# DeltaNet heads of a 1-core transformer kernel: the triangular inversion on packed 64x64 blocks, keys left unscaled

## The reference, cut to what matters

```python
def l2norm(t):
    return t * lax.rsqrt(jnp.sum(t * t, axis=-1, keepdims=True) + EPS)

def gated_delta_scan(q, k, v, g, beta, s0, with_output):
    ...   # q is l2norm(q) * 128 ** -0.5, k is l2norm(k)
    gc = jnp.cumsum(to_chunks(g), axis=-1)
    decay = jnp.exp(jnp.where(incl, gc[..., :, None] - gc[..., None, :], -jnp.inf))
    kb = kc * bc[..., None]
    lmat = jnp.where(pos[:, None] > pos[None, :],
                     jnp.einsum('nbhid,nbhjd->nbhij', kb, kc) * decay, 0.0)
    rhs = jnp.concatenate([vc * bc[..., None], kb * jnp.exp(gc)[..., None]], axis=-1)
    sol = lax.linalg.triangular_solve(lmat, rhs, left_side=True, lower=True, unit_diagonal=True)
    ...
    def step(s, inp):
        v_new = u_i - jnp.einsum('bhcd,bhde->bhce', w_i, s)
        s_next = s * gl_i[..., None, None] + jnp.einsum('bhcd,bhce->bhde', kd_i, v_new)
        ...   # o = qd_i s + qk_i v_new
def finish(o, z):
    o = o * lax.rsqrt(jnp.mean(o * o, axis=-1, keepdims=True) + EPS) * onorm.astype(f32)
    y = o.astype(z.dtype) * jax.nn.silu(z).reshape(b, l, nh, HEAD_DIM)
```

## Time and profile before

| | |
|---|---|
| time, median of 3 runs (lowest, highest) | 4285.75 us (4284.77, 4294.96) |
| span of the profiled execution | 4288.7 us (no separate device time is given for it) |
| PE busy | 3886.8 us (91%) |
| DVE, ACT, POOL busy | 2858.3 us (67%), 1920.1 us (45%), 855.2 us (20%) |
| mean granted clock of PE over the span | 0.943 |

### The profile page before, as it was taken

The page is one execution under the profiler, slowest core; times in us unless marked ns, Lnnn a source line. Parts: engine busy times, 40 slices in busy tenths (PEclk is TensorE's granted clock), DMA queues, the critical chain, the costliest instruction groups (busy, mean ns, idle before and its releaser), DMA issues. The chain is left out here.

```text
span 4288.7 us, 52316 instructions
## 1 busy us (share of the span) xinstructions
PE 3886.8 (91%) x18886; PEld 3096.0 (72%) x18886; DVE 2858.3 (67%) x3428; ACT 1920.1 (45%) x2304; POOL 855.2 (20%) x436
## 2 busy tenths in 40 slices
PE   8998998979988989799989998799999797999996
PEld 6755787637557777488888887578887575888885
DVE  6764775468758763455555555489998454999996
ACT  2052432332023322534444444377777223777774
POOL 1100000003000000122222221135554000455552
PEclk8999999989999999899999998899999798999998
DMA  6321454207313542100000001299997414999994
GB/s 220 141 97 40 157 177 141 91 30 251 112 59 118 177 157 61 29 20 20 18 13 13 15 19 41 102 391 355 356 373 283 155 43 167 379 365 360 368 358 155
DMA packets 222417, 689.14 MB, mean 161 GB/s; under 512 B 27699, under 2 KB 107699, under 8 KB 197076
## 3 DMA queue, kind: packets, MB, share of 16 engines
q1 hardware_dynamic: 192000, 648.17, 41.3%
q10 hardware_dynamic: 11572, 22.45, 1.5%
q0 software_dynamic: 18720, 16.84, 1.1%
HBM read 697.86 MB, written 40.89 MB: 172 GB/s over the span
## 5 line engine op out<-in xcount | busy, mean ns | idle before, releaser
L584 PE MATMUL psum<-work_rounded 128*128 128x512 f32 x3504 | 1163.4, 402 | 83.5 <-DVE work_rounded L578 31.1
L578 DVE TENSOR_TENSOR ring_rounded<-ring,work_rounded 128x2048 fp32r<-128x2048 f32 (+1 forms) x445 | 816.0, 1836 | 369.2 <-ACT work_rounded L573 282.6
L584 PEld LDWEIGHTS psum<-work_rounded 128*128 128x128 f32 x3504 | 667.9, 192 | 252.8 <-issue 98.8
L584 PE MATMUL psum<-work_rounded,fixed_rounded 128*128 128x512 f32 x2544 | 781.3, 401 | 17.6 <-POOL ring_rounded L578 6.0
L584 PE MATMUL psum<-work_rounded,ring_rounded 128*128 128x512 f32 (+1 forms) x1824 | 727.2, 399 | 0.0
L573 ACT ACTIVATE work_rounded<-ring 128x1024 fp32r<-128x1024 f32 x204 | 214.6, 1057 | 949.6 <-PE psum L584 692.7
L3334 ACT ACTIVATE work_rounded<-ring 128x2048 fp32r<-128x2048 f32 x256 | 490.8, 1919 | 201.0 <-PE psum L584 172.6
L584 PEld LDWEIGHTS psum<-work_rounded,fixed_rounded 128*128 128x128 f32 x2544 | 482.6, 190 | 135.8 <-issue 13.2
L584 PE MATMUL psum<-fixed_rounded,work_rounded 128*128 128x512 f32 (+1 forms) x1088 | 433.5, 398 | 0.0
L584 PEld LDWEIGHTS psum<-work_rounded,ring_rounded 128*128 128x128 f32 x1824 | 351.3, 193 | 79.3
L578 DVE TENSOR_TENSOR work_rounded<-work,work_rounded 128x2048 fp32r<-128x2048 f32 (+1 forms) x196 | 337.8, 1733 | 29.2 <-ACT work_rounded L3334 23.3
(11 more groups left out here) (371 smaller groups left out, 5868.8 us busy)
## 6 DMA issues: line engine op xcount, KB each, us to landing
ring<-in_w SPq DMA_DIRECT2D x128, 2048.0 KB, 8.4
work<-in_w SPq DMA_DIRECT2D x64, 2048.0 KB, 8.2
ring<-in_mod_w SPq DMA_DIRECT2D x24, 2048.0 KB, 8.5
ring<-in_ada_w SPq DMA_DIRECT2D x24, 2048.0 KB, 7.9
ring<-in_ffn_w_in SPq DMA_DIRECT2D x44, 1024.0 KB, 7.6
ring<-in_ffn_w_out SPq DMA_DIRECT2D x10, 2048.0 KB, 7.9
ring<-in_w_in_a SPq DMA_DIRECT2D x32, 512.0 KB, 6.4
ring<-in_hy_w_in SPq DMA_DIRECT2D x6, 2048.0 KB, 8.6
```

The costliest lines, as they stand in the source:

```text
L578: return eng.tensor_tensor(c.rounded(v), v, c.rounded(v_high), ALU.subtract)
L584: ins = pe.matmul(out, c.rounded(w), c.rounded(x), start=(start and i == 0), stop=(stop and i == 2))
```

## The change

Tiles of 128x128 in the inversion become two diagonal blocks of 64x64 kept side by side: a chunk is held as 128 partitions x 64 columns (`compact`, 128x384 for the six chunks), which is all that levels 1 to 5 need; the off-diagonal corner is kept in an array of its own (`L_X`) for level 6. So masks, L, T and TT are half as wide. `masked` becomes 12 products of 64x64 by 64x64 per lane (upper and lower half in turn) in place of 6 of 128x128. Their results go by two ACT copies of 64 partitions each into the diagonal blocks of a 128x128 matrix A whose other blocks hold zeros, and `update` uses that whole matrix as the stationary operand with 64 moving columns. For v = 5 each chunk has a 64x64 product ahead of the whole one. Level 6 is 64x64 for all six chunks.

Keys and queries are no longer scaled by their lengths: the sums of squares go into a coefficient beta / |k|^2 (`coef`) that scales L and, in the scan, vn (L2658 gets a scale per partition); the turned values are multiplied by |k| on POOL; q's length goes into the epsilon of the output's norm. The spread products L2372 and L2476 and `unit` go. The order changes too: the opening of head h + 1 (`*_begin`) comes ahead of the closing of head h (`tensor_spread`, `vector_finish`), the squares are taken before the last tile is evacuated, and POOL's order is new. Before the first head DVE sets the zero blocks once.

```diff
         same = (j // (2 * s)) == (i // (2 * s))
...
-    masks = -np.stack(levels, 1).reshape(P, 14 * P).astype(np.float32)
+    masks = np.stack([m[0:HALF, 0:HALF] for m in levels] + [np.eye(HALF)], 1).astype(np.float32)
+    masks[:, 0:2 * WHOLE + 2] *= -1
+    masks = np.concatenate([masks, masks]).reshape(P, -1)
...
-        self.wait_mixed(pe, h, "cols", 1)
+        self.wait(pe, h, "conv", 5)
+        self.wait(pe, h, "silu", 5)
+        self.turn_values(pe, h)
         decays(0)
-        self.wait(pe, h, "unit", 2)
-        self.wait(pe, h, "turned_out", 2)
-        for t in range(NTC, NTA):
-            ins = pe.matmul(c.ps[:, 3, P * (t - NTC):P * (t - NTC) + P], self.k[:, P * t:P * t + P],
-                            self.q[:, P * (t - NTC):P * (t - NTC) + P], start=True, stop=True)
-        ins.then_inc(s["kk"], 1)
         for t in range(NTA):
             cols = slice(P * t, P * t + P)
-            pe.matmul(c.pair(6, KEYS)[:, cols], self.k[:, cols], self.k[:, cols], start=True, stop=True)
...
-        self.wait(pe, h, "qk", 1)
-        rates(0, 2)
+            ins = pe.matmul(c.pair(6, KEYS)[:, cols], self.k[:, cols], self.k[:, cols], start=True, stop=True)
+        ins.then_inc(s["gram"], 1)
+        self.lengths(pe, h)
         decays(1)
-        self.wait(pe, h, "grown", 2)
-        rates(1, 4)
+        self.turn_keys(pe, h)
+        self.wait(pe, h, "turned_out", 2)
+        if last is not None:
+            self.tensor_sums(pe, last)
+        for t in range(NTC, NTA):
+            ins = pe.matmul(c.ps[:, 4, P * (t - NTC):P * (t - NTC) + P], self.k[:, P * t:P * t + P],
+                            self.q[:, P * (t - NTC):P * (t - NTC) + P], start=True, stop=True)
+        ins.then_inc(s["qkp"], 1)
...
+    def tensor_sums(self, pe, h):
+        c = self.c
+        self.wait(pe, h, "osq", 1)
+        for t in range(NT):
...
+    def tensor_spread(self, pe, h):
+        c = self.c
+        self.wait(pe, h, "oroot", 1)
+        for t in range(NT):
+            ins = pe.matmul(c.ps[:, 5, P * t:P * t + P], self.root[:, t:t + 1].to_broadcast([P, P]),
...
         def place(l):
 
             self.wait(pe, h, "tt", l + 1)
-            for t in range(NTA):
-                pe.matmul(c.pair(4 * l + 2, KEYS)[:, P * t:P * t + P], ident, self.lane(l, L_TT, NTA, P)[:, t, :],
-                          start=(t % 4 == 0), stop=True, skip_group_check=True)
+            self.wait(pe, h, "grown", l + 1)
+            pe.matmul(c.ps[:, 2 * l + 1, 0:COMPACT], c.const("ident"), self.lane(l, L_TTC, COMPACT),
+                      start=True, stop=True, skip_group_check=True)
...
         def masked(v, l):
...
+            for t in range(NTA):
+                if v > WHOLE:
+                    ins = pe.matmul(out[rows, t, :], self.compact(l, L_X)[cols, t, :], T_[cols, t, :], start=True, stop=True)
+                    continue
+                for half in self.halves():
+                    ins = pe.matmul(out[half, t, :], M[half, t, :], T_[half, t, :], start=True, stop=True)
+            ins.then_inc(s["a"], 1)
...
+        def update(v, l):
...
-        def update(v, l):
...
-            for t in range(NTA):
...
-                if t and v == LEVELS - 1:
-                    ins = pe.matmul(corner[:, t, :], A[rows, t, half], TT[rows, t, rows], start=False, stop=True,
-                                    skip_group_check=True)
+                if v > WHOLE:
+                    ins = pe.matmul(at[cols, t, :], A[rows, t, rows], whole[rows, t, rows], start=True, stop=True)
                     continue
                 if v == WHOLE:
-                    pe.matmul(c.pair(4 * l, KEYS)[:, cols], TT[:, t, :], A[:, t, :], start=True, stop=True)
-                ins = pe.matmul(c.pair(4 * l + 2, KEYS)[:, cols], A[:, t, :], TT[:, t, :], start=False, stop=True,
-                                skip_group_check=True)
-            ins.then_inc(self.s["x"], 1)
+                    pe.matmul(at[cols, t, :], TT[cols, t, :], A[cols, t, cols], start=True, stop=True)
+                ins = pe.matmul(out[:, t, :], A[:, t, :], TT[:, t, :], start=False, stop=True, skip_group_check=True)
+            ins.then_inc(s["x"], 1)
...
+    def scalar_begin(self, act, h, last):
...
-
-        def grow(l):
-
-            act.activation(self.lane(l, L_KBG, KEYS), c.pair(4 * l, KEYS), ACT.Exp).then_inc(s["grown"], 1)
-
+            act.activation(self.lane(l, L_KBG, KEYS), c.pair(2 * l, KEYS), ACT.Exp).then_inc(s["grown"], 1)
+
+        if last is not None:
+            self.keep_o(act, last)
+        self.wait(act, h, "cols", 1)
         decay(0)
-        grow(0)
+        self.keep_keys(act, h)
         decay(1)
-        grow(1)
+        act.activation(self.eg, self.gcum, ACT.Exp).then_inc(s["eg"], 1)
+        if last is not None:
+            self.square_o(act, last)
+        self.wait(act, h, "coef", 1)
+        act.activation(self.nk, self.sums[:, 0:NTA], ACT.Sqrt).then_inc(s["nk"], 1)
+        if last is not None:
+            self.deviate_o(act, last)
...
         def keep_masked(v, l):
 
+            rows = self.corner(l)[0]
+            A = self.lane(l, L_A, NTA, P)
             self.wait(act, h, "a", 2 * v - 1 + l)
-            act.activation(self.lane(l, L_A, KEYS), c.pair(4 * l, KEYS), ACT.Copy).then_inc(s["a_out"], 1)
+            for half in ((rows,) if v > WHOLE else self.halves()):
+                ins = act.activation(A[half, :, half], self.banked(2 * l)[half], ACT.Copy)
+            ins.then_inc(s["a_out"], 1)
 
         def keep_update(v, l):
 
+            whole = self.lane(l, L_TT, NTA, P)
+            rows, cols = self.corner(l)
             if v < WHOLE:
                 self.wait(act, h, "upd", 2 * v + 1 + l)
+                ins = act.activation(self.compact(l, L_TTC), self.banked(2 * l + 1), ACT.Copy)
+            elif v == WHOLE:
+                self.wait(act, h, "x", 2 * v - 1 + l)
+                for half in (cols, rows):
+                    ins = act.activation(whole[half, :, half], self.banked(2 * l + 1)[half], ACT.Copy)
             else:
                 self.wait(act, h, "x", 2 * v - 1 + l)
-            act.activation(self.lane(l, L_TT, KEYS), c.pair(4 * l + 2, KEYS), ACT.Copy).then_inc(s["a_out"], 1)
+                ins = act.activation(whole[cols, :, rows], self.banked(2 * l)[cols], ACT.Copy)
+            ins.then_inc(s["a_out"], 1)
 
...
-            act.activation(self.st(l, 2), c.ps[:, 2 * l, P:2 * P], ACT.Copy).then_inc(s["vn_out"], 1)
+            act.activation(self.st(l, 2), c.ps[:, 2 * l, P:2 * P], ACT.Copy, scale=self.coef[:, l, t:t + 1])\
+                .then_inc(s["vn_out"], 1)
...
+    def vector_begin(self, dve, h, last):
...
+        self.keep_values(dve, h)
+        if last is not None:
+            self.vector_add(dve, last)
+        self.wait(dve, h, "lens", 1)
...
+        def first(l):
...
+            self.wait(dve, h, "flat", l + 1)
+            self.wait(dve, h, "gram", 1)
+            for half in self.halves():
+                dve.tensor_tensor(L_[half], m[half, :, half], g[half, :, half], ALU.mult)
+            dve.drain()
+            dve.tensor_tensor(L_, L_, c_, ALU.mult)
+            dve.drain()
+            dve.tensor_tensor(TT, L_, self.mask(0, l).unsqueeze(1).to_broadcast([P, NTA, HALF]), ALU.mult)
+            dve.drain()
+            dve.tensor_tensor(TT, TT, c.view(G_MASK + MASKS - HALF, HALF).unsqueeze(1).to_broadcast([P, NTA, HALF]), ALU.add)
+            dve.drain().then_inc(s["tt"], 1)
+            dve.transpose(self.lane(l, L_T, COMPACT), self.lane(l, L_TTC, COMPACT))
+            dve.drain().then_inc(s["upd"], 1)
+            rows, cols = self.corner(l)
+            dve.tensor_tensor(self.compact(l, L_X)[cols], m[cols, :, rows], g[cols, :, rows], ALU.mult)
+            dve.drain()
+            dve.scalar_tensor_tensor(out=self.compact(l, L_X)[cols], in0=self.compact(l, L_X)[cols], scalar=-1.0,
+                                     in1=c_[cols], op0=ALU.mult, op1=ALU.mult).then_inc(s["cross"], 1)
+            dve.tensor_copy(self.kd[:, l, :], m[:, :, last])
...
+        first(0)
+        first(1)
+        self.wait(dve, h, "qkp", 1)
...
+    def vector_finish(self, dve, h):
+
+        c, s = self.c, self.s
+        self.wait(dve, h, "ostd", 1)
+        dve.reciprocal(self.root, self.root)
+        dve.drain().then_inc(s["oroot"], 1)
+        dve.tensor_scalar(self.q_eps, self.sums[:, NTA:NTA + NT], P * RMS_EPS, None, ALU.mult)
+        self.wait(dve, h, "ospread", 1)
+        dve.tensor_tensor(self.o, self.o, c.ps[:, 5, :], ALU.mult)
+        dve.drain()
```

More of the change, by code:

```diff
@@ L48 @@
 GRID_W = 64
+HALF = P // 2
 HID = 64
@@ L2315, in vector @@
         self.gates.keep_sums(dve)
-        self.keep_values(dve, 0)
-        self.unit(dve, 0, 0)
+        dve.drain()
         self.load_cols(dve, 0)
-        with dve.Fori(0, DHEADS - 1) as h:
-            self.vector_head(dve, h, True)
-        self.vector_head(dve, DHEADS - 1, False)
+        for l in range(2):
+            rows, cols = self.corner(l)
```

(71 more changed lines are left out.)

319 lines of the change are left out of this document (148 added, 171 removed).

## The result

The changed kernel takes 4327.31 us (median of 4 runs, 4315.45 to 4338.68) against 4285.26 of the kernel before in the same set: a ratio of 1.0087, 95% interval 1.006 to 1.0114. It is 42 us slower; 4334 was forecast. The profiled execution, the longest of the four, has a span of 4336.8 us against 4288.7, so 48 us are to be found in the trace.

A forecast was written before the change was run, and what follows sets the result against it. PE bounds the scan and fills levels 2 to 5; the opening is a chain. Terms sum to +5.9 us a head, times 8 = +47, plus 1 once: span 4337, so 4334 us; own range 4300 to 4375, wider 4240 to 4395.

The forecast's parts named there:

- Opening: From the SiLU of z to `place`: shorter chain, 22.3 us instead of 26.4, -4.1 a head.
- (d): Opening: no shorter, for instance because the closing's chain ends last; +4 us a head, 4366 us; chance 0.09.
- Level 1: First inversion level: two lanes 10.4 us against 11.0, but starting at half clock, so 12 us, +1 a head.
- Levels 2 to 4: Inversion levels: masked 3.0 plus update 2.8 us, 5.8 a level against 5.56, +0.7 for three.
- (a): Inversion levels: upper and lower 64x64 products run beside each other; a level takes 5.0 us, total 4297; chance 0.22.
- Level 5: Alternating narrow and wide update: 11.1 us against 8.3, +2.8, and about 4 more from the clock falling to half.
- Level 6 and scan: After level 5, per head: level 6 +0.5 us, the scan's first steps at half clock +1.0 us.
- (b): Level 5 update: shape changes cost nothing in the long run and the clock stays up; 4243 us; chance 0.17.
- (c): Whole inversion: clock is half throughout because narrow products run all through it; 4500 us; chance 0.05.

The follow-up runs named there:

- the experiment with the late spread: Changed kernel with the closing's spread products and two last VectorE instructions moved behind level 1 of the next head; 4273.89 us, ratio 0.9959.
- filled kernel: Changed kernel plus ten unread 128x512 products per head where PE waits in the opening; 4312.67 us, ratio 1.0062.
- the order half by half: Changed kernel with each masked product doing its six upper 64x64 products first, then its six lower ones; 4459.98 us, ratio 1.0405.
- grouped order: Changed kernel with level 5's update doing its six narrow products of a lane first, then its six whole ones; 4266.59 us, ratio 0.9952.

## Why the prediction came out, step by step

**The total** was right, 4334 against 4327, and so was the sign, but that it came so near is in part luck. In head 3 the opening, level 1, levels 2 to 4 and the scan came out 3.5, 1.9, 1.6 and 0.4 us above the forecast, levels 5 and 6 3.2 and 0.8 below it: 3.4 too long in sum. The mean over the heads met the forecast (116.3 against 116.4) because head 0, which the forecast does not treat apart, is 6.5 us shorter than before. What the forecast had right is why the change loses: the alternating update of level 5 and the clock that falls in it.

**Opening** (-4.1 forecast, -0.6 measured in head 3): wrong. Its rival (d), no shorter opening because the closing ends last, is what happens, at 3.5 us above the forecast where (d) had 4; the experiment with the late spread shows it by shortening the opening by 8.1 us. (d)'s total, 4366, did not come, since level 5 came out shorter. The working did have the reciprocal and the spread at the chain's end; its sizes were short. VectorE's reciprocal ends at 2170.33, 22.0 us behind the SiLU, against 20.4: in its second lane VectorE waits 0.75 us for ScalarE, and two instructions take 1.22 and 0.99 us where they take 0.86 and 0.55 in the first. The spread, at half clock as forecast, takes 0.3 more. And the working missed the turn of the loop, 1.65 us of `issue` in head 3. Before, the turn lies ahead of the first decays, where `issue` shows less:

```profile
2150.77 1.60 PE L2469 MATMUL psum<-fixed,work 128*128 128x128 f32 x12 [0.62 <-issue]
```

The opening does gain in head 0, which has no closing: `place` stands 11.3 us behind the SiLU, against 24.0 before.

**Level 1** (+1, measured +2.9): the half clock was counted for part of the first lane, and it lasts all of level 1 in heads 1 to 7. At full clock, in head 7 of the filled kernel, level 1 is 8.7: the work itself had become cheaper than the forecast 10.4 (whose terms add up to 5.3 a lane, not 5.2).

**Levels 2 to 4** (+0.7, measured +2.3): rival (a)'s mechanism is true. A level at full clock takes 5.02 us, (a)'s 5.0 and not 5.8, and the order half by half shows that opposite blocks overlap. The gain, 3 x (5.56 - 5.02) = 1.6 us, is more than eaten by 11.8 us at half clock, which the forecast did not have here.

**Level 5** (+6.8, measured +3.6): the mechanism is right, its size was too large. A chunk costs 0.62 (forecast 0.68; the wide part holds PE 0.36 us and not 0.42); masked costs 2.2 and not 3.0; the clock falls in the update, as forecast, but halfway, and costs 12 x 0.62 = 7.4 against the measured 9.8: 2.4 and not 4. The grouped order, whose update takes 4.6 us at full clock, shows both parts.

**Level 6 and scan** (+0.5 and +1.0, measured -0.3 and +1.4): half clock in both, as forecast; the grouped order gives 1.4 and 2.9 back.

**The other rivals.** (b), on the other side, is refuted as it stands: a chunk costs 0.62 us and not under 0.45, a change of shape 0.14, and the clock does fall. The grouped order, with few such changes, goes to 4267, on (b)'s side of no change. (c) did not come about here, yet it did in the half-by-half order, so it was not far off.

**Not tried.** No run packs the tiles and still scales keys and queries, or leaves them unscaled on whole tiles, so these two parts of the change are not priced apart.

## What to carry to other kernels

For small f32 products like these, count changes of operand shape and weight loads on PE before arithmetic: keep products of one shape together, let 64x64 products on opposite diagonal blocks alternate, and do not pad a block-diagonal matrix to 128x128 to save an instruction. Look for what holds the first product of a stage back, the closing of the stage before and the turn of the loop among it, and move it behind. When work gets smaller, read the granted clock beside the busy time: a stage that is cheaper at full clock can come out longer.

## What was not expected of the hardware

- Two 64x64 products on opposite diagonal blocks (0.035 us a record in turn) beat one product with a 128x128 weight load (0.115 us a record), although they issue twice the records: 1.92 against 2.86 us at full clock.
- A change between 64x64 and 128x128 operands costs PE 0.14 us, and the update of level 5 that makes twelve of them a lane ends at half clock in all eight heads, where the one that makes two keeps 1.00 in all eight.
- The turn of the loop ahead of `place` leaves PE idle for 1.65 (after) and 2.60 us (filled waits) by the profile's `issue`. In the filled kernel `place` behind it took 1.64 us, at half clock, and 0.81 in head 7, without a turn.
- With PE busy for 28.6 of 28.6 us in levels 2 to 4 (products half by half), the clock was 0.50 throughout; with the same products in turn (kernel after) it came back to full within these levels.
